# Scan of the state-space mixer: the samples' B and C spread over the partitions by a small store and a broadcast load

## What is computed

```
xbc = silu(causal_dwconv(xpad, conv_w, conv_b))            # x: 2048 channels, B: 8 groups x 128, C: 8 groups x 128
xs, bm, cm = split(xbc)
# for each sample, group, head of the group (4) and channel of the head (64); n = 0..127 is the state's last axis
new_state = state * exp(dt * a) + (x * dt)[channel] * bm[group, n]
y         = sum over n of cm[group, n] * new_state         # a sample has one token: this is its whole scan
out       = rmsnorm_of_group((y + d_skip * x) * silu(z)) * norm_w @ w_out
```

## Time and profile before

| | |
|---|---|
| median of 3 runs | 3417.2 us (3415.84 to 3420.82) |
| profiled execution, its own time | 3418.3 us |
| its span | 3416.5 us |
| mean granted share of TensorE's clock | 0.968 |
| instructions in the span | 56741 |
| busy share PE / DVE / ACT / POOL | 95% / 45% / 33% / 35% |
| the scan's eight groups | about 1729 to 2533 us of the span |

### The profile page before, as it was taken

How to read it: one execution, slowest core, us unless ns; L and a number is a source line. 1 busy time by engine, 2 the same in 40 slices (tenths; PEclk the granted TensorE clock), 3 DMA queues, 4 the chain that set the end, 5 groups by cost and what they waited for, 6 DMA issues and landing times. The chain is left out here.

```text
span 3416.5 us, 56741 instructions
## 1 busy us (share of the span) xinstructions
PE 3243.2 (95%) x20604; PEld 3060.4 (90%) x20604; DVE 1527.9 (45%) x2686; ACT 1143.8 (33%) x2132; POOL 1206.0 (35%) x889
## 2 busy tenths in 40 slices
PE   7889988988999999999999999999899999999998
PEld 6569984667999999999898989898889999999998
DVE  3699993523221212122557677767742212122122
ACT  3512214623321213132445555445532412122222
POOL 2206844312312222223365455566443221222222
PEclk9989999968999999999999999999999999999999
DMA  4218646022311111112222233221441111111111
GB/s 136 54 31 144 194 160 223 8 78 90 45 49 44 48 48 44 49 43 82 56 83 93 82 94 100 80 94 57 150 138 49 43 50 43 49 43 49 43 49 69
DMA packets 344008, 263.90 MB, mean 77 GB/s; under 512 B 52134, under 2 KB 308150, under 8 KB 341910
## 3 DMA queue, kind: packets, MB, share of 16 engines
q1 hardware_dynamic: 327926, 232.18, 22.7%
q0 software_dynamic: 8192, 19.13, 1.6%
q10 hardware_dynamic: 7776, 11.09, 1.5%
HBM read 219.43 MB, written 44.76 MB: 77 GB/s over the span
## 5 line engine op out<-in xcount | busy, mean ns | idle before, releaser
L234 POOL TENSOR_TENSOR w_low_sb<-w_loaded_sb,w_high_sb 128x1024 fp32r<-128x1024 f32 (+1 forms) x278 | 569.3, 2055 | 1550.9 <-ACT w_high_sb L226 1527.1
L252 PE MATMUL psum<-act_high_sb,w_high_sb 128*128 128x344 f32 (+1 forms) x2400 | 770.0, 321 | 10.6 <-PEq L985 5.7
L252 PE MATMUL psum<-act_low_sb,w_high_sb 128*128 128x344 f32 (+1 forms) x2400 | 768.3, 320 | 0.0
L252 PE MATMUL psum<-act_high_sb,w_low_sb 128*128 128x344 f32 (+1 forms) x2400 | 768.1, 320 | 0.0
L252 PE MATMUL psum<-second_high_sb,w_high_sb 128*128 128x344 f32 x1728 | 553.3, 320 | 0.5 <-PEq L2382 0.5
L252 PE MATMUL psum<-second_low_sb,w_high_sb 128*128 128x344 f32 x1728 | 551.9, 319 | 0.0
L252 PE MATMUL psum<-second_high_sb,w_low_sb 128*128 128x344 f32 x1728 | 551.9, 319 | 0.0
L252 PEld LDWEIGHTS psum<-act_high_sb,w_high_sb 128*128 128x128 f32 (+1 forms) x2400 | 451.1, 188 | 12.1 <-issue 10.8
L252 PEld LDWEIGHTS psum<-act_high_sb,w_low_sb 128*128 128x128 f32 (+1 forms) x2400 | 451.4, 188 | 0.4
L252 PEld LDWEIGHTS psum<-act_low_sb,w_high_sb 128*128 128x128 f32 (+1 forms) x2400 | 451.1, 188 | 0.4
L226 ACT CAST w_high_sb<-w_loaded_sb 128x1024 fp32r<-128x1024 f32 (+1 forms) x230 | 239.5, 1043 | 518.6 <-PE psum L252 498.0
(11 more groups left out here) (434 smaller groups left out, 4812.9 us busy)
## 6 DMA issues: line engine op xcount, KB each, us to landing
w_loaded_sb<-in_w_up SPq DMA_DIRECT2D x64, 512.0 KB, 4.0
w_loaded_sb<-in_w_down SPq DMA_DIRECT2D x64, 512.0 KB, 3.6
w_loaded_sb<-in_w_in_odd SPq DMA_DIRECT2D x48, 512.0 KB, 4.0
key_pages_sb<-in_cache_k SPq DMA_DIRECT2D x64, 256.0 KB, 3.1
ecay_sum_spread_sb<-decay_sum_scratch SPq DMA_DIRECT2D x8, 2048.0 KB, 9.8
w_loaded_sb<-in_w_in_even SPq DMA_DIRECT2D x28, 512.0 KB, 3.9
value_pages_sb<-in_cache_v SPq DMA_DIRECT2D x52, 256.0 KB, 4.9
gated_scratch<-gated_sb POOLq DMA_DIRECT2D x8, 1032.0 KB, 4.4
```

The lines of the kernel that those rows point to most:

```text
L234: ins = self.nc.gpsimd.tensor_tensor(self.wl[:, par, k, 0:width], self.wf[:, par, k, 0:width], self.wh[:, par, k, 0:width].bitcast(F32), A ...
L252: ins = nc.tensor.matmul(out, w[:, par, k, 0:width], a[:, k, cols], start=n == 0, stop=n == 3 * KT - 1)
```

## The change

B and C of the 8 samples go another way to all partitions. Once `conv_out` of C is there, SyncE stores the 8 columns of B and the 8 of C turned to a scratch in HBM (`sample_b_c_scratch`, 4 KB each), where a sample's 128 values lie side by side, and loads 4 KB of it to each of the 128 partitions (512 KB): B by SyncE behind the state loads, C by POOL at k = 3. `spr` takes the place of `dg` in SBUF. POOL's diagonals and TensorE's products with ones are gone, VectorE reads SBUF in place of PSUM. In SyncE's stream unit 1 now comes before the state loads, which stand behind the wait for `conv_out` and the two stores. Two waits that `spread` held move to `sample_sum` and `turn_state`.

```diff
@@ in mamba_groups
-    dg = B.take("diagonals_sb", [P, NS, P])
+    spr = B.take("sample_b_or_c_sb", [P, NS, P])
...
+    B.bc_scratch = nc.dram_tensor("sample_b_c_scratch", (G, 2, NS, P), F32, kind="Internal").ap()
...
+    s_bcs, s_spr = B.sem("sample_b_c_stored"), [B.sem("sample_b_loaded"), B.sem("sample_c_loaded")]
...
+    def load_spread(eng, g, i):
+        eng.wait_ge(s_bcs, g * 32 + 32)
+        B.hold(eng)
+        eng.dma_start(spr[:].rearrange("p b n -> p (b n)"),
+                      bass.AP(tensor=B.bc_scratch.tensor, offset=g * (2 * NS * P) + i * NS * P,
+                              ap=[[0, P], [1, NS * P]])).then_inc(s_spr[i], 16)
@@ SyncE, part(g, nx, more), behind the load of bc
+                    if nx is not None:
+                        load_unit(nx, 1)
+                    sp.wait_ge(S["conv_out"], g * 4 + 4)
+                    B.hold(sp)
+                    with nc.allow_non_contiguous_dma("B and C of eight samples, turned"):
+                        for i in range(2):
+                            sp.dma_start(B.bc_scratch[bass.ds(g, 1), i].rearrange("o b n -> n (o b)"),
+                                         post[:, 2 + i, SEQ:TOK]).then_inc(s_bcs, 16)
                     sp.wait_ge(s_sto, g * (16 * NS))
                     sp.wait_ge(S["sample_gated"], g)
...
                     for b in range(NS):
                         sp.dma_start(st[:, b], ...).then_inc(s_st, 16)
+                    load_spread(sp, g, 0)
                 if nx is not None:
-                    for e in range(1, 6):
+                    for e in range(1 if g is None else 2, 6):
                         load_unit(nx, e)
...
-                    sp.wait_ge(S["diagonal"], G * 2)
+                    sp.wait_ge(s_spr[1], 16 * G)
@@ POOL
-            def diagonals(j):
-
-                for b in range(0, NS, 4):
-                    ins = nc.gpsimd.tensor_tensor(dg[:, b:b + 4], B.ident[:].unsqueeze(1).to_broadcast([P, 4, P]),
-                                                  post[:, j, SEQ + b:SEQ + b + 4].unsqueeze(2).to_broadcast([P, 4, P]), ALU.mult)
-                ins.then_inc(S["diagonal"], 1)
...
-                if g is not None:
-
-                    pool.wait_ge(S["conv_out"], g * 4 + 4)
-                    pool.wait_ge(S["sample_gated"], g)
-                    diagonals(2)
...
                         pool.wait_ge(S["outer"], g + 1)
                         pool.wait_ge(S["sample_decayed"], g + 1)
-                        diagonals(3)
+                        load_spread(pool, g, 1)
@@ TensorE
-            def spread(g, m):
-
-                await_group(pe, S["diagonal"], g, 2, m + 1)
-                if m == 0:
-                    pe.wait_ge(S["state_rows"], g)
-                    pe.wait_ge(S["sample_scaled"], g)
-                for a in range(2):
-                    ins = nc.tensor.matmul(B.psum[:, 6 + a, :], B.ones[:],
-                                           dg[:, 4 * a:4 * a + 4, :].rearrange("p b n -> p (b n)"), start=True, stop=True)
-                ins.then_inc(S["spread"], 1)
...
-                if k == 2:
-                    spread(g, 0)
-                if k == 5:
-                    spread(g, 1)
...
             def sample_sum(g):
                 pe.wait_ge(S["sample_gated"], g + 1)
+                pe.wait_ge(S["sample_mean"], g)
...
             def turn_state(g):
+                pe.wait_ge(S["state_rows"], g)
@@ VectorE, outer and sample_y
-                await_group(dve, S["spread"], g, 2, 1)
+                dve.wait_ge(s_spr[0], g * 16 + 16)
                 for c in range(2):
-                    ins = nc.vector.tensor_tensor(tmp[:, c], B.psum[:, 6:8, :].rearrange("p a (b n) -> p (a b) n", b=4),
+                    ins = nc.vector.tensor_tensor(tmp[:, c], spr[:],
...
-                await_group(dve, S["spread"], g, 2, 2)
+                dve.wait_ge(s_spr[1], g * 16 + 16)
...
-                    step(nc.vector.tensor_tensor(tmp[:, c], B.psum[:, 6:8, :].rearrange("p a (b n) -> p (a b) n", b=4),
+                    step(nc.vector.tensor_tensor(tmp[:, c], spr[:],
```

More of the change, by code:

```diff
@@ L2747, in mamba_groups @@
              "exps", "cb_masked", "scores", "x_dt", "x_decayed", "x_d", "state_decayed", "state", "gated",
-             "square_sums", "rstd", "gated_scaled", "gated_turned", "gated_stored_col", "diagonal", "spread", "outer",
+             "square_sums", "rstd", "gated_scaled", "gated_turned", "gated_stored_col", "outer",
              "sample_state", "sample_gated", "sample_sum", "conv_rows_turned", "conv_rows_kept", "state_turned",
```

## The result

The changed kernel takes 3508.6 us (median of 4 runs, 3506.5 to 3515.3) against 3418.3 us of the kernel before on the same chip (4 runs, 3415.8 to 3420.8): ratio 1.0267, 95% interval 1.025 to 1.0285, or +90 us. Forecast were +25 us, 3442 us and a range up to 3500: the direction was right, the size far off.

What follows compares the result with a forecast made beforehand. TensorE, busy 95%, was taken as the bound, with POOL right behind at two places a group. Seven groups at +2.8 us (19.6) and the closing 5.4 made +25, 3442 us; range from 3396, less 2, to 3500.

Steps and rivals of the forecast that it cites:

- The store price: Two turned stores on SyncE: 13.0 us to land, half the 26.0 of four earlier query stores, in proportion to packets.
- the 49 GB/s: Rate of all queues together while small packets are under way; the state load was taken to crawl at it.
- C's load, issued by POOL: Load issued near the second diagonals' place, some 15 us before VectorE uses it: cost 0.
- VectorE's operand: Moves from PSUM to SBUF: counted 0, at most tenths of a microsecond slower, covered by TensorE's tiles.
- What is queued behind: SyncE's later loads, B and weight units 2 to 5, and C's load: all hidden, 0.
- The state's landing: State load lands 15.1 us after conv_out, POOL wants it at +11.4: TensorE 3.7 us late a group, bounds 0 and 12.6.
- First spread: First products with ones (B) removed: worth 0, TensorE standing about 1.7 us more at the same place; at most 1.9.
- Second spread: Second products with ones (C) removed: 1.7 us of TensorE plus 0.9 wait for x_decayed, 2.6 a group, bounds 1.7 and 3.5.
- stores land at once: Rival: state in time, seven groups win 2.6 each and the closing 3.4: -21.6, 3396 us; chance 0.26.
- The clock: One dip of TensorE's granted clock a group, behind its long stand: 1.7 us, bounds 0 and 3.4.
- The closing group: Output projection's raw loads come later, TensorE opens 8.8 us later, two spreads give back 3.4: net +5.4.
- The rival with a price of 26 us: Stores cost nearly 26 us, state 12.6 late, two clock dips: +112, 3529 us; chance 0.14 with what lies between.

Runs made afterwards that it cites:

- e5: Changed kernel with state loads ahead of the stores, and convolution rows in the tile's last two blocks, VectorE waiting for them at chunk 6: 3461.9 us.
- e14: e6 plus one broadcast load of decay sums, issued by POOL right ahead of its four additions: 3446.6 us.
- e15: Changed kernel with C's load issued by SyncE between two weight loads instead of by POOL: 3468.5 us.
- e12: e10 with POOL's decay of the samples' state put behind the low half, at chunk 2: 3408.1 us.
- e3: Changed kernel with the eight state loads back ahead of the stores and the wait for conv_out: 3476.6 us.
- e4: Changed kernel with convolution rows in the tile's last two blocks, VectorE waiting for their stores at chunk 6 instead of its first gate: 3514.9 us.
- e6: e3 without stores and loads of B and C, VectorE multiplying by a constant tile in SBUF: 3413.5 us.
- e8: Changed kernel with B and C turned by TensorE and stored in 16 rows of 512 bytes, behind early state loads: 3454.7 us.
- e10: e8 with C's load issued by SyncE between two weight loads instead of by POOL: 3414.2 us.
- e2: Changed kernel with the two stores not turned, 32-byte packets instead of 4-byte ones, B and C in wrong order: 3456.7 us.
- e9: e8 with POOL waiting after each of its four additions for that addition's end: 3426.5 us.
- e11: e6 plus one more POOL multiplication of 128x256 right ahead of the four additions, no DMA: 3420.0 us.
- e13: Kernel before with one edit, POOL's decay of the samples' state at chunk 2, behind the low half: 3404.6 us.

## Why the prediction was wrong, point by point

- **The store price, right.** Landed at +13.1 was taken, +14.0 measured (13.8 us from the first issue). It isn't a constant: with the state loads ahead of the stores SyncE goes on 11.2 us after the issue (e5). Scaling the queries' stores by the number of packets held. So did the 49 GB/s in kind: 23 GB/s here.
- **"C's load, issued by POOL", counted at 0: this step failed.** Its price is 40 us (3508.6 to 3468.5 with SyncE issuing it), 27.5 to 28.5 of it waiting, as e14's table and the fall from 43.5 to 15.0 in e15's show, the rest clock. I had asked only when C's load lands, not what its issue does to POOL's next instructions and to an engine that works in SBUF beside them. What it hit was x_dt, which the change doesn't touch.
- **"VectorE's operand", counted at 0 and at most tenths of a microsecond: failed too, by less.** Beside POOL's decay the two products of `outer` take 3.9 to 4.0 us from SBUF (4.34 beside a low half) and 2.36 from PSUM, and from SBUF they slow the decay by 2 us. In the seven groups TensorE doesn't wait for it (in group 1 it stands for w_low anyway); it shows in the closing group, as a part of the 5.6 us for `x_sb` against 1.3, and in e12.
- **"What is queued behind": failed too.** I followed SyncE's own queue (B, weight units) and stopped there. The packets delay every queue's transfers, POOL's stores of convolution rows among them, and VectorE's first gate waits for their landing. The packets alone cost +48. e3, e4 and e5 show why one remedy is not enough: with either of rows and state mended the other is still late.
- **The state's landing, taken 3 us too early.** +15.1 expected, POOL started its decay at +18.1, after the rows had held it up to +17 anyway; so 6.7 us behind the +11.4 of the prediction, and not 3.7. TensorE's stand at w_low was 6.35 us, 6.4 expected: right by luck, since 3.06 us of another stand lay ahead of it, 9.4 together.
- **First spread worth 0: right as a wait.** With nothing late the wait at that place was 2.7 us, as expected (1.0 + 1.7); the dip of the clock behind it had no price where nothing is late.
- **Second spread worth 2.6 a group: right as time on TensorE, wrong as time of the kernel.** Without stores and loads of B and C (e6) -5.6 us came out where -21.6 were forecast for "stores land at once". The wait for x_decayed went and so did the products, but I gave no price in that rival to the clock, nor to the closing group's stand for `x_sb`.
- **The clock, undersized.** 1.7 us a group taken; about 6.5 in the group shown, which has three stands with a dip behind each where one had been expected.
- **The closing group: the opening nearly right, the rest not.** From the convolution's end (2505.33) to TensorE's opening at 2529.15 there are 23.8 us, 13.3 before: +10.5, 8.8 expected. Net +13 instead of +5.4: no late gate is in it (VectorE's gate 0 at 2534.90 waits for no DMA), but TensorE's second stand of 5.63 us, 1.3 before, takes back more than the 3.4 of the two spreads (some 1.7 of its growth is the empty place of the first of them, which had stood ahead of it).

By the terms of the sum: seven groups at +2.8 came out at +11.05, which is 58 us of the miss, the closing group 7.6. The rival with a price of 26 us came near in time (3529) for a wrong reason.

The step that failed is thus the list of who is touched by the new transfers: the sum priced them at SyncE's queue and the state alone (+2.8 a group), and the runs show +48 us by POOL's stores of convolution rows and other transfers, and +40 by POOL's own issue.

What stays open: why the DMA issue makes POOL's run indivisible, and whether it is any DMA issue or this form. Between e8 and e10, 27.6 of the 40.5 us are the wait; that the other 13 are all clock is argued, from 0.957 against 0.964, and not shown.

## What to carry to other kernels

Stores of 4-byte packets are not priced by their own landing: list every transfer of every queue that is under way in the next 14 us, and who waits for each, output stores whose source is reused above all. A DMA that GpSimd issues just ahead of a run of its own SBUF work can keep a VectorE operation with two SBUF operands out for the whole run: let SyncE issue it. Moving an operand of VectorE's from PSUM to SBUF can cost both engines where GpSimd works in SBUF beside it. And before taking work off a busy TensorE, see whether the place will be idle instead; a one-line reordering of the engine behind it may be worth more than the removal.

## What the runs showed of the hardware

- 2,048 packets of 4 bytes took 13.8 us to land (11.2 in e5) and held all queues together to 23 GB/s; as packets of 32 bytes (e2), or in 16 rows of 512 (e8), the same 8 KB delayed nothing that shows in the seven groups (w_low 22.7 to 22.8 us, no wait for convolution rows or state).
- With a DMA issue of GpSimd's just ahead, a VectorE multiplication of 128x256 with both operands in SBUF stood for the rest of a run of six GpSimd instructions, 5.7 us (e14 and six other kernels); without one 0.66 to 1.34 us, and the GpSimd operations gave way (5.63 instead of 4.98 us for four). A wait of GpSimd's between the pieces ended it (e9, 0.83 us in the same group). The Trainium skill, "SBUF — State Buffer", section "SBUF: two separate sides", has GpSimd and a VectorE operation with two SBUF inputs lock one pair of ports, for one whole instruction. The runs agree without the DMA issue: 0.66 us in e11 is less than the 0.42 of x_dt alone and one addition of 1.2 us together. With the issue the hold went over several instructions; here page and measurement differ, and the measurement decides.
- Two of VectorE's wide products (128x1024 each) took 2.36 us from a tile in SBUF while GpSimd was idle (e10), and 3.93 to 4.34 while GpSimd worked in SBUF (e12, the changed kernel), where GpSimd's four operations took 6.03 in place of 4.07 (e12). From PSUM the products took 2.36 and the operations 4.07 at the same time (e13).
